# Head 0's weights and the first eight V rows, moved forward into the query projection

## The reference

```
q = (h @ w_peer_q)                       # 2048 -> 8 heads x 2 halves x 128
s1, s2 = q[:, :, 0] @ keys0.T, q[:, :, 1] @ keys1.T       # 128 scores each
v1, i1 = top_k(s1, 16);  v2, i2 = top_k(s2, 16)
top_s, idx = top_k(all 256 sums v1 + v2, 16)              # 16 of 16384 experts
gate = softmax(top_s)
a = peer_u[idx] . h                      # one dot of 2048 per picked expert
y = sum over heads, picks of gate * gelu(a) * peer_v[idx]
```

## Time and profile before

| | us |
|---|---|
| median of 3 runs | 2757.74 |
| lowest, highest | 2751.84, 2759.45 |
| profiled execution | 2753.93 |
| its span | 2752.2 |
| PE busy | 2449.5 (89%) |
| DVE busy | 1433.6 (52%) |
| POOL busy | 1063.3 (39%) |
| ACT busy | 353.3 (13%) |
| gathers and other POOL transfers | 725.64 MB |
| SP transfers | 192.20 MB |

### The profile page before, as it was taken

The page is one execution under the profiler, slowest core; times in us unless marked ns, Lnnn a source line. Parts: engine busy times, 40 slices in busy tenths (PEclk is TensorE's granted clock), DMA queues, the critical chain, the costliest instruction groups (busy, mean ns, idle before and its releaser), DMA issues.

```text
span 2752.2 us, 27802 instructions
## 1 busy us (share of the span) xinstructions
PE 2449.5 (89%) x9109; PEld 1570.1 (57%) x9109; DVE 1433.6 (52%) x2306; ACT 353.3 (13%) x781; POOL 1063.3 (39%) x953
## 2 busy tenths in 40 slices
PE   9999999989999999999997787776999597777777
PEld 7888887868766678888885233332434142233333
DVE  3465566962322223002478877884554656555543
ACT  2111000003222211001112101111011011111110
POOL 1265566020122200000056565654444564446542
PEclk9999999999999999999998999998989899999999
DMA  7698898594799965447498999999999999999998
GB/s 225 229 342 312 317 345 318 192 345 145 268 345 350 354 235 187 140 150 244 129 368 341 422 419 417 415 416 422 421 410 422 413 420 418 420 418 416 417 421 372
DMA packets 305904, 919.33 MB, mean 334 GB/s; under 512 B 15738, under 2 KB 196050, under 8 KB 236756
## 3 DMA queue, kind: packets, MB, share of 16 engines
q0 software_dynamic: 122448, 725.64, 65.5%
q1 hardware_dynamic: 183332, 192.20, 21.3%
HBM read 909.08 MB, written 8.72 MB: 333 GB/s over the span
## 4 chain that ended last, share of the span: by engine, by line
PE 31%; DMA 23%; DVE 15%; issue 14%; POOL 13%; POOLq 3%; ACT 1%; DVEq 0%; SPq 0%; ACTq 0%
DMA sb_bregion<-in_peer_u_dram,sb_ring 13%; PE ps L770 12%; PE ps L782 6%; PE ps L676 4%; DMA sb_mkv<-in_peer_u_dram,sb_ring 3%; POOL sb_ring L447 3%; DVE sb_bregion L1968 3%; DMA sb_S<-in_peer_u_dram,sb_ring 3%; POOL sb_mkv L447 3%; PE ps L1021 2%; PE ps L872 2%; POOL sb_bregion L548 2%; POOLq L438 2%; POOL sb_wring L548 2%; DVE sb_mkv L1968 1%
## 5 line engine op out<-in xcount | busy, mean ns | idle before, releaser
L1021 PE MATMUL ps<-sb_wring,sb_ring 128*128 128x512 f32 x992 | 456.9, 610 | 84.9 <-DMA sb_wring<-in_peer_v_dram,sb_ring 84.3
L676 PE MATMUL ps<-sb_hT,sb_wring 128*128 128x264 f32 x1792 | 409.4, 389 | 7.1 <-DMA sb_wring<-in_w_in_dram 7.1
L1968 DVE CUSTOM_DVE_ANT_0 sb_bregion<-sb_bregion,sb_rows 128x2048 f32<-128x2048 f32 x128 | 293.5, 2293 | 214.4 <-DMA sb_bregion<-in_peer_u_dram,sb_ring 207.2
L1021 PEld LDWEIGHTS ps<-sb_wring,sb_ring 128*128 128x128 f32 x992 | 186.1, 194 | 354.5 <-issue 260.6
L770 PE MATMUL ps<-sb_hT,sb_wring 128*128 128x264 f32 x1536 | 366.5, 389 | 13.9 <-ACTq L1173 10.6
L676 PEld LDWEIGHTS ps<-sb_hT,sb_wring 128*128 128x128 f32 x1792 | 340.3, 192 | 66.8 <-ACTq L1150 4.6
L770 PEld LDWEIGHTS ps<-sb_hT,sb_wring 128*128 128x128 f32 x1536 | 287.7, 190 | 77.7 <-issue 27.3
L1021 PE MATMUL ps<-sb_oreg,sb_ring 128*128 128x512 f32 x496 | 238.9, 632 | 72.8 <-DMA sb_oreg<-in_peer_v_dram,sb_ring 50.9
L1021 PE MATMUL ps<-sb_hT,sb_ring 128*128 128x512 f32 x496 | 231.6, 613 | 55.0 <-DMA sb_hT<-in_peer_v_dram,sb_ring 50.2
L548 POOL DMA_INDIRECT sb_bregion<-in_peer_u_dram,sb_ring x132 | 186.4, 1412 | 215.5 <-DVEq L1359 181.1
L1021 PEld LDWEIGHTS ps<-sb_oreg,sb_ring 128*128 128x128 f32 x496 | 97.1, 202 | 213.4 <-issue 147.2
(11 more groups left out here) (374 smaller groups left out, 2776.6 us busy)
## 6 DMA issues: line engine op xcount, KB each, us to landing
sb_wring<-in_w_in_dram SPq DMA_DIRECT2D x52, 2048.0 KB, 12.7
sb_ring<-in_cache_k_dram POOLq DMA_DIRECT2D x64, 512.0 KB, 7.0
sb_mkv<-in_cache_k_dram POOLq DMA_DIRECT2D x64, 512.0 KB, 6.7
sb_mkv<-in_cache_v_dram POOLq DMA_DIRECT2D x48, 512.0 KB, 7.1
sb_rows<-in_cache_v_dram POOLq DMA_DIRECT2D x47, 512.0 KB, 7.2
sb_wring<-in_w_mem_kv_dram SPq DMA_DIRECT2D x8, 2048.0 KB, 10.3
sb_wring<-in_w_o_dram SPq DMA_DIRECT2D x8, 2048.0 KB, 8.1
sb_S<-in_cache_v_dram POOLq DMA_DIRECT2D x22, 512.0 KB, 6.9
```

Of the source, the lines that this page charges most:

```text
L676: last = mm(ps[:, (2 * r + c) % 4, 0:NT], wring[:, r, k, c * P:(c + 1) * P], rhs[:, k, :], start=(k == 0), stop=(k == KC - 1))
L1021: last = mm(ps[:, 4 * t + q, :], diag[:, k % 4, :], e_slots[v % ER][:, q * 512:(q + 1) * 512], start=False, stop=q_stop, skip_group_check= ...
L1968: st(V.tensor_tensor_reduce(out=u_slots[n % UR], in0=u_slots[n % UR], in1=h2, scale=1.0, scalar=0.0, op0=ALU.mult, op1=ALU.add, accum_out= ...
```

## The change

Three edits. `v_before` gets a list of eight U rows after which the first eight V rows are issued; from there the even rule holds where it is larger. On ACT, `winners(0)` goes behind part 5 of the projection and `activations(0)` behind part 11 (both stood after part 17). On DVE, `weigh(0)` goes from the first dot of group 2 (dot 32) to the seventh of group 1 (dot 22).

```diff
+        FIRST_V = [18, 20, 28, 29, 31, 32, 33, 34]
         def v_before(n):
-            return max(0, (n - V_LEAD + 1) * (V_SLOTS - V_LEFT) // (U_SLOTS - V_LEAD))
+            even = (n - V_LEAD + 1) * (V_SLOTS - V_LEFT) // (U_SLOTS - V_LEAD)
+            return max(sum(first <= n for first in FIRST_V), even)
...
+            stage_part(0)
+            stage_part(1)
+            keep_scores(0)
+            keep_scores(1)
+            for i in range(2, len(PQ_PARTS)):
+                stage_part(i)
+                keep_scores(i)
+                if i == 5:
+                    winners(0)
+                if i == 11:
+                    activations(0)
             v = 0
             for g in range(2 * PH):
                 diagonals(v, v_before(u_slot(g, TOPK - 1)))
                 v = v_before(u_slot(g, TOPK - 1))
-                activations(g)
+                if g:
+                    activations(g)
                 if g + 1 < 2 * PH:
                     winners(g + 1)
...
-                    if j == 0 and g == 2:
+                    if j == 6 and g == 1:
                         weigh(0)
```

More of the change, by code:

```diff
@@ L1283, in keep_scores @@
                 act.sem_inc(s["rows_taken"], 1)
[L1285 to L1291, removed]
             def activations(g):
@@ L1332, in diagonals @@
                         diagonal(v)
-            winners(0)
+            stage_part(0)
[9 more added lines that the diff above has]
+                    activations(0)
             v = 0
```

## The result

| | before | changed |
|---|---|---|
| median of 6 runs, us | 2753.94 | 2765.82 |
| lowest, highest | 2747.83, 2759.45 | 2762.34, 2768.01 |
| profiled execution | 2753.93 | 2764.36 |
| its span | 2752.2 | 2762.7 |

The change makes the kernel slower: ratio 1.0039, 95% interval [1.0029, 1.0049], about 11 us.

The account below looks back on a forecast made before the run. Transfers were taken as the bound from 1550 us on, so only transfer time lost earlier counts. Terms -2.5 - 1.5 + 9.6 + 0.5 = +6.1 us gave 2760.0 profiled and a 2763.8 us median; range 2752 to 2771.

Parts of the forecast that it names:

- The bound: From 1550 us transfers set the pace; the end moves by transfer time lost before, 14.5 us in the kernel before.
- Hole A: Transfer gap at 1458 to 1470 us, after dot 19 while DVE routes head 2: shrinks, -2.5 us (0 to -5.0).
- 1470 to 1510: Stretch in us with U rows alone queued: V rows from U28 on deepen the queue, -1.5 us (0 to -4.2).
- Hole B: New transfer gap after dot 35 while DVE routes head 3, four gathers queued: +9.6 us (+7 to +12).
- After it: U40 to U42, following the new gap after dot 35, issued one per dot: +0.5 us (0 to 0.9).
- The second way, over DVE: Check by the chain of dots: dot 42 at 1558.4 us against 1550.52, +7.9 us.
- Weight blocks and POOL: Early V gathers would not wait for weight blocks in their slots; nearest margin V4's, 10 us or more.
- Head 0's weights: Exponential and Gelu moved into the projection on ACT, weigh to dot 22 on DVE: cost 0.
- A: Rival: POOL's issue becomes the bound as early gathers fall among dots; +11.2 us, about 2769, chance 0.17.
- B: Rival: V rows fill the transfer gaps and little opens after dot 35; about -9 us, 2749, chance 0.15.
- C: Rival: same transfers, gains and losses cancel; within 2 us, 2757, chance 0.10.
- D: Rival: ACT's wait for dot 15 at the Gelu holds the projection; +8 us or more, 2766, chance 0.03.

Follow-up runs that it names:

- e8: Changed kernel with only four early V rows (after U20, U22, U23, U23), then the even rule unchanged; ratio 0.9996 to the kernel before.
- e6: Changed kernel, same eight early V rows, but seven added to the even rule from U34, fading by U133; ratio 1.0000 to the kernel before.
- e2: Changed kernel with the list of early V rows emptied, leaving only the ACT and DVE moves; ratio 1.0008 to the kernel before.
- e5: Changed kernel with four early V rows (after U20, U22, U23, U23), four added from U34, fading by U133; ratio 0.9974 to the kernel before.
- e4: Changed kernel, same eight early V rows, seven added to the even rule from U34 at lower pace (237 over 230); ratio 1.0032 to before.

## Why the prediction was right or wrong

The forecast was +6.1 us on a profiled execution, 2763.8 us for the median. The time came out at 2765.82, inside the range and inside its own range of 2758 to 2768, but the closeness flatters it: the median of before, 2757.74 in three runs, is 2753.94 in six, and the measured step is about +11 (10.4 in the profiled executions, 10.7 by the ratio, 11.9 by the medians), not +6. Counted from 2753.94 the sum would have given 2760.0. So the close number is luck; the step itself came out at or just above the sum's own upper bound of +10.4. I had called "within 0.3%" likelier (0.58) than slower (0.30); 0.39% is slower.

Step by step, by the stretches above and the earlier trace rows:

*The bound.* Right. From 1550 us on the share is 1.01 and 418 GB/s in both kernels, and the difference is made before: lost 23.8 against 14.5 us, +9.3; dot 16 comes 1.1 us later because the projection starts 2.0 us later, in work ahead of all edits. Together 10.4 of the span's 10.5 us.

*Hole A, -2.5.* 8.1 us before; now 10 x (421-154)/421 = 6.3 us, moved to 1464: -1.8. Dot 19 comes 4.6 us later, of it 1.1 from the start, so the V rows push it by 3.5 us and not by the 2.5 of the prediction; U23, dot 20 and U24 move with it. Two V rows are 5.0 us of transfers, and 5.0 - 3.5 = 1.5 is near what was measured.

*1470 to 1510, -1.5.* 4.2 us before; now 0.8 (1474 to 1480) and 0.9 (1480 to 1510): -2.5. Inside the bounds.

*Hole B, +9.6.* The mechanism came where the prediction put it, the size was short: 16 x (421-113)/421 = 11.7 us. Its end is right: transfers resume at 1544 - 2 x 229/421 = 1542.9, 19.6 us after dot 35's start (the prediction's hole and backlog add to 19.5). Its beginning is early: at 1528 + 2 x (365+299)/421 = 1531.2 the four rows are through, 7.9 us after dot 35's start and not 9.9. I had let the dot start with the last byte of its row; the row that stands next is by then nearly through. That this gap is about 2 us is read off this one place: in e8 the six gathers (14.9 us) ended 14.5 us after the dot's start, which fits a gap of half a microsecond. What sets it stays open. The prediction had considered this case, and with the wrong sign: a dot that starts 2.5 us after its row landed has less backlog behind it, so the hole would be 9.6 + 2.5 = 12.1 us, while the prediction put this case down as its lower bound of 7.

*After it, +0.5.* 16 x (421-374)/421 = 1.8 us in 1544 to 1560. In proportion this term was the most under-sized: V8 is issued at 1547.67, and until then one gather goes out per dot.

The sum as measured: -1.8 - 2.5 + 11.7 + 1.8 = +9.2. The second way, over DVE, forecast dot 42 7.9 us later; it came 11.3 later (1561.84), 1.1 of it from the start. As a check it is sound only because both kernels have issued the same eight V rows by dot 42, so that the delay is transfer time lost. In e6 dot 42 comes 12.6 us later at no cost, with six more V rows moved.

*Weight blocks and POOL.* No V row waited for one, as said: V0 was issued straight behind U18. The nearest margin was V6's and not V4's: part 17 is over at 1483.3, V6 is issued at 1500.34. What I left out is the reverse: V0 and V1 share the transfers with the projection's block 7, and PE waited for that block, 0.49 us ahead of part 16. It cost nothing here, since the projection's end (1486.97, 2.6 us later, 2.0 of them the later start) is ahead of what needs it.

```profile
1467.78 7.39 PE L998 MATMUL ps<-sb_hT,sb_rows 128*128 128x264 f32 x32 [0.49 <-DMA sb_rows<-in_w_peer_q_dram]
```

*Head 0's weights, 0.* Right for the projection: it takes 132.9 us in place of 132.3, and the wait above is most of the difference. For the whole run 0 lies inside e2's interval, which reaches to 0.17%. The Gelu's table load stands in ACT's pause, and the copy behind it follows without another load:

```profile
1443.10 0.58 ACT L1284 ACTIVATE sb_conv<-ps 128x128 f32<-128x128 f32 x3 [6.99 <-PE ps L980]
1443.79 1.28 ACT L1291 ACT_TABLE_LOAD   x1
1445.08 0.21 ACT L1291 ACTIVATE sb_ring<-sb_ring 128x16 f32<-128x16 f32 x1
1445.41 0.39 ACT L1275 ACTIVATE sb_zst<-ps 128x264 f32<-128x264 f32 x1
```

*The rivals.* A forecast +11.2, nearly the number that came, but not by its mechanism: 1480 to 1510 runs at 408 GB/s, so POOL's issue is no bound while dots wait for rows. A gather occupies POOL 0.94 us while DVE waits or routes and 2.2 to 3.0 us among dots (the prediction's 2.2 to 2.4 leaves out rows such as 2.83 and 2.97); that decides only in the catch-up after a hole. The Trainium skill ("GPSIMD Engine Reference", 8. Key points) states that GpSimd contends for SBUF with VectorE instructions that have two SBUF inputs. The trace agrees with that in the single gather; no run here tests the cause. B (holes fill, -9) failed for this list; its point, four U slots can't carry DVE's pause and seven U rows bring no other work, was the argument against it. With four other early rows and V rows kept behind the pause, e5 reaches B's size: -8.3. C (no effect) is excluded by the interval. D needed dot 15 more than 5.7 us later; it came 1.3 us later (1435.00), and ACT got to the Gelu at 1443.79.

## What to carry to other kernels

Where transfers are the bound and one queue issues two streams of rows, the order is worth the transfer time lost, here to within about 5 us. Count for each pause of the consumer how many gathers stand behind it (here 19.6 us pass from the start of the last dot until transfers resume; nine gathers of 2.49 us covered that, eight nearly), and never take rows out of a place that had enough to fill one that had too few. Prefetched rows must be added to the stream and given back slowly, not borrowed from what follows at once. A lead also has to be gone before the next place where its consumer stops: with three rows left it blocked the shared queue there.

## What the runs showed that I had not expected

A lead of seven V rows costs nothing for 600 us (1560 to 2100 us run at 418 GB/s, as before) and then, with three rows of it left, 14 us at one wait (28.04 us, e4). And a stream of dots can run 12.6 us late at no cost (e6), while in the changed kernel 11.3 us of lateness at the same dot are a loss: in a kernel bound by transfers the time at which an engine reaches a step says little unless one also counts what has been moved by then.
